# Value, key and query projections of a hybrid encoder layer as three products over high and low halves, the low halves by GpSimd

## The reference

```
xn = rmsnorm(h, norm_mix_g)
proj = xn @ w_in                      # 2048 x 3584
a = proj[..., :2048]                  # gated convolution (GLU)
q, k, v = 1024, 256 and 256 columns   # attention, rope on q and k
glu = a[..., :1024] * sigmoid(a[..., 1024:])
y = depthwise conv of glu, 31 taps    # then layernorm, silu
mn = rmsnorm(mem, norm_mem_g)         # 256 memory tokens
mk, mv = mn @ w_ck, mn @ w_cv
```

## Time and profile before

| what | us |
|---|---|
| median of 3 runs | 2055.32 |
| lowest and highest run | 2044.23 and 2055.69 |
| the profiled execution | 2047.77 |
| its span, first to last instruction | 2046.0 |

### The profile page before, as it was taken

How to read it: one execution, slowest core, us unless ns; L and a number is a source line. 1 busy time by engine, 2 the same in 40 slices (tenths; PEclk the granted TensorE clock), 3 DMA queues, 4 the chain that set the end, 5 groups by cost and what they waited for, 6 DMA issues and landing times. The chain is left out here.

```text
span 2046.0 us, 29568 instructions
## 1 busy us (share of the span) xinstructions
PE 1981.8 (97%) x11192; PEld 1765.1 (86%) x11192; DVE 1530.7 (75%) x2436; ACT 858.1 (42%) x857; POOL 718.3 (35%) x504
## 2 busy tenths in 40 slices
PE   7999998999899999999999999999999999999997
PEld 6987776998799999999999889988888888888886
DVE  5988745456678788989988987567677777778875
ACT  4340136334334554455454435433434343334343
POOL 2010110220726677587787875011001011114300
PEclk9999998999899999999999999999999999999999
DMA  5464393443344787788888787779998989998983
GB/s 207 164 193 141 116 400 137 153 168 123 127 137 156 247 275 268 272 281 286 274 272 298 265 306 283 294 274 348 340 343 328 343 326 349 364 360 345 372 314 136
DMA packets 101226, 531.27 MB, mean 260 GB/s; under 512 B 19376, under 2 KB 21568, under 8 KB 45792
## 3 DMA queue, kind: packets, MB, share of 16 engines
q1 hardware_dynamic: 71552, 408.93, 55.8%
q0 software_dynamic: 24304, 106.45, 14.4%
q10 hardware_dynamic: 5296, 14.98, 1.9%
HBM read 491.34 MB, written 38.14 MB: 259 GB/s over the span
## 5 line engine op out<-in xcount | busy, mean ns | idle before, releaser
L889 DVE TENSOR_TENSOR wl<-raw,wh 128x2048 fp32r<-128x2048 f32 x310 | 712.4, 2299 | 287.1 <-ACT wh L519 275.5
L519 ACT ACTIVATE wh<-raw 128x2048 fp32r<-128x2048 f32 x310 | 593.3, 1915 | 572.5 <-DMA raw<-in_v 408.4
L1537 PE MATMUL acc<-xhl,wh 128*128 128x448 f32 x2048 | 648.9, 377 | 12.2 <-DVE wl L889 12.2
L1538 PE MATMUL acc<-xhl,wl 128*128 128x224 f32 x2048 | 542.8, 265 | 0.0
L1537 PEld LDWEIGHTS acc<-xhl,wh 128*128 128x128 f32 x2048 | 386.7, 189 | 44.7 <-DVE wl L889 14.6
L1538 PEld LDWEIGHTS acc<-xhl,wl 128*128 128x128 f32 x2048 | 393.2, 192 | 0.0
L2025 POOL DMA_INDIRECT G<-gsum,cell x224 | 348.2, 1554 | 99.7 <-issue 74.8
L1514 PE MATMUL acc<-xhl,wh 128*128 128x288 f32 x768 | 231.7, 302 | 14.8 <-DVE wl L925 14.2
L1515 PE MATMUL acc<-xhl,wh 128*128 128x288 f32 x768 | 228.4, 297 | 0.0
L1516 PE MATMUL acc<-xhl,wl 128*128 128x288 f32 x768 | 227.9, 297 | 0.0
L1514 PEld LDWEIGHTS acc<-xhl,wh 128*128 128x128 f32 x768 | 146.5, 191 | 18.2 <-DVE wl L925 14.2
(11 more groups left out here) (306 smaller groups left out, 2638.8 us busy)
## 6 DMA issues: line engine op xcount, KB each, us to landing
raw<-in_u SPq DMA_DIRECT2D x128, 1024.0 KB
raw<-in_v SPq DMA_DIRECT2D x128, 1024.0 KB
raw<-in_w_mix SPq DMA_DIRECT2D x28, 1024.0 KB
G<-zero SPq DMA_DIRECT2D x16, 1024.0 KB, 13.8
raw<-in_w_out SPq DMA_DIRECT2D x16, 1024.0 KB
raw<-in_w_pq SPq DMA_DIRECT2D x16, 1024.0 KB
gin<-G SPq DMA_DIRECT2D x32, 512.0 KB
h<-hbg ACTq DMA_DIRECT2D x32, 448.0 KB
```

Of the source, the lines that this page charges most:

```text
L519: act.activation(wh[:, n % 4], raw[:, n % 4], ACT.Copy).then_inc(hi_done, 1)
L889: dve.tensor_tensor(wl[:, n % 4], raw[:, n % 4], wh[:, n % 4].bitcast(F32), ALU.subtract).then_inc(lo_done, 1)
L1537: pe.matmul(acc[:, s, 0:2 * NU], wh[:, s, j, :], xu[:, j, 0:2 * NU], start=(j == 0), stop=False)
L1538: ins = pe.matmul(acc[:, s, 0:NU], wl[:, s, j, :], xuh[:, j, :], start=False, stop=(j == DT - 1))
```

## The change

The plain float32 products of the 12 value, key and query slots become three products over `wh`, `wl`, `xh` and `xl`. ScalarE makes the 12 high halves, which were not made before, GpSimd makes the 12 low halves with one subtraction of 128 x 2048 elements each, into `wl`. `xg` and its 16 copies are gone. The memory tokens are loaded into a tile of their own where `xg` was; the squares and the scaled copy `memg` lie over `wh` and are made when slots 9, 10 and 11 of the stage have been used. GpSimd's sums of convolution tiles move between its subtractions, and its two cache loads wait for the scaled memory tokens.

```diff
-            memsq, memT = sb(o, "memsq", [P, DT, MEM]), sb(o, "memT", [P, DT, MEM])
+            memsq, memg = sb(o, "memsq", [P, DT, MEM]), sb(o, "memg", [P, DT, MEM])
...
-                    xg = sb(o1, "xg", [P, DT, N])
+                    memT = sb(o1, "memT", [P, DT, MEM])
...
+        vkq_lo = sem("vkq_lo")
...
-            def glu_iteration(i, first=False, last=False):
+            def glu_iteration(i, first=False):
                 for s in range(4):
-                    if not (last and s >= 4 - AHEAD):
-                        hi_next(GLU0, i, s)
-                    if last:
-                        for t in range(4 * s, 4 * s + 4):
-                            act.activation(xg[:, t, :], hT[:, t, :], ACT.Copy, scale=par[:, Q_GMIX + t:Q_GMIX + t + 1]).then_inc(xg_ready, 1)
+                    hi_next(GLU0, i, s)
...
             act.wait_ge(lo_done, VKQ0)
-            act.sem_inc(hi_done, OUT0 - VKQ0)
+
+            for n in range(12 - AHEAD):
+                hi_next(VKQ0, 0, n)
+            act.wait_ge(vkq_lo, 12)
+            act.sem_inc(hi_done, OUT0 - MEM0)
+            act.wait_ge(slot_used, VKQ0 + 10)
             for n in range(4):
                 at = slice(4 * n, 4 * n + 4)
                 act.wait_ge(mem_in[n], 16)
                 act.activation(memsq[:, at, :], memT[:, at, :], ACT.Square).then_inc(mem_sq, 1)
-                act.wait_ge(mem_sq, n + 1)
+            for n in range(4):
+                act.wait_ge(slot_used, VKQ0 + 11 + n // 2)
                 for m in range(4 * n, 4 * n + 4):
-                    ins = act.activation(memT[:, m, :], memT[:, m, :], ACT.Copy, scale=par[:, Q_GMEM + m:Q_GMEM + m + 1])
+                    ins = act.activation(memg[:, m, :], memT[:, m, :], ACT.Copy, scale=par[:, Q_GMEM + m:Q_GMEM + m + 1])
                 ins.then_inc(mem_ready, 1)
 
+            act.wait_ge(mem_sq, 4)
+            act.wait_ge(mem_ready, 4)
...
             for n in range(12):
-                pe.wait_ge(raw_in[n % 4], 16 * (VKQ0 // 4 + n // 4 + 1))
+                pe.wait_ge(vkq_lo, n + 1)
                 pe.wait_ge(acc_free, VKQ0 + n + 1)
                 for j in range(DT):
-                    if n == 0 and j % 4 == 0:
-                        pe.wait_ge(xg_ready, j + 4)
-                    ins = pe.matmul(acc[:, n % 4, 0:N], raw[:, n % 4, j, :], xg[:, j, :], start=(j == 0), stop=(j == DT - 1))
+                    pe.matmul(acc[:, n % 4, 0:N], wh[:, n % 4, j, :], xh[:, j, :], start=(j == 0), stop=False)
+                    pe.matmul(acc[:, n % 4, 0:N], wh[:, n % 4, j, :], xl[:, j, :], start=False, stop=False)
+                    ins = pe.matmul(acc[:, n % 4, 0:N], wl[:, n % 4, j, :], xh[:, j, :], start=False, stop=(j == DT - 1))
                 ins.then_inc(slot_used, 1)
...
+            def weight_lo(n):
+
+                pool.wait_ge(hi_done, VKQ0 + n + 1)
+                pool.tensor_tensor(wl[:, n % 4], raw[:, n % 4], wh[:, n % 4].bitcast(F32), ALU.subtract).then_inc(vkq_lo, 1)
+
+            for n in range(AHEAD):
+                weight_lo(n)
             pool.wait_ge(acc_free, VKQ0 + 4)
             pool.wait_ge(hist_zero, 1)
             pool.wait_ge(hist_in, 16)
             pool.dma_start(dr["nconv_p"], glu[:, :, NP_:NP_ + HIST]).then_inc(early_out, 16)
             pool.dma_start(dr["nconv_s"], glu[:, :, XW - HIST:XW]).then_inc(early_out, 16)
-            for t in range(1, CT - 1):
+
+            def ln_part(t):
+
                 pool.wait_ge(conv_dve, t + 1)
...
+            for n in range(AHEAD, 12):
+                weight_lo(n)
+                if n % 2 == 1:
+                    ln_part(n // 2)
+            for t in range(12 // 2, CT - 1):
+                ln_part(t)
             pool.wait_ge(slot_used, MEM0)
+            pool.wait_ge(mem_ready, 4)
```

More of the change, by code:

```diff
@@ L322, in build @@
         x_in = [sem(f"x_in{n}") for n in range(4)]
-        xg_ready = sem("xg_ready")
         mem_sq, mem_ready, mem_stat = sem("mem_sq"), sem("mem_ready"), sem("mem_stat")
@@ L559, in _ @@
             glu_iteration(0, True)
-            with act.Fori(1, 3) as i:
+            with act.Fori(1, 4) as i:
                 glu_iteration(i)
-            glu_iteration(3, last=True)
             act.wait_ge(lo_done, VKQ0)
-            act.sem_inc(hi_done, OUT0 - VKQ0)
+            for n in range(12 - AHEAD):
[3 more added lines that the diff above has]
+            act.wait_ge(slot_used, VKQ0 + 10)
             for n in range(4):
@@ L1656, in mem_part @@
                         pe.wait_ge(mem_ready, j // 4 + 1)
-                    ins = pe.matmul(acc[:, 2 + m % 2, 0:MEM], raw[:, m % 4, j, :], memT[:, j, :], start=(j == 0), stop=(j == DT - 1))
+                    ins = pe.matmul(acc[:, 2 + m % 2, 0:MEM], raw[:, m % 4, j, :], memg[:, j, :], start=(j == 0), stop=(j == DT - 1))
                 if part == 3:
```

## The result

| | before | changed |
|---|---|---|
| median us | 2055.07 (4 runs, 2044.23 to 2055.69) | 2090.69 (4 runs, 2088.91 to 2093.68) |
| profiled execution: span | 2046.0 | 2089.0 |
| rope's first instruction | 228.01 | 265.42 |

The ratio is 1.0187, with a 95% interval of 1.0167 to 1.0206: slower by 1.7 to 2.1%, some 38 us. It is estimated from all runs; the two medians alone differ by 35.6 us. The number on record was 2090.

What follows compares the result with a forecast made beforehand. TensorE set the pace, but VectorE ended the stage: 12 x 4.45 us lost to GpSimd's subtractions less 13.75 of waits is 39.7; 2047.8 + 39.7 + 2.2 (clock) = 2090 us, range 2072 to 2108.

Steps and rivals of the forecast that it cites:

- The point to follow: End of the value, key and query stage: rope's start, 228.01 us before, was put at 267.7, 39.7 us later.
- the short pairs: Overlapping VectorE and GpSimd instructions before the change: VectorE lost GpSimd's duration less about 0.15 us, as 0.65 of 0.81.
- TensorE off the path: In the 12 slots: products fall from 7.78 to 6.29 us a slot; gain beyond VectorE's 13.2 us of waits doesn't count.
- What is queued behind: Behind GpSimd's subtractions: five convolution sums and two DMA issues move back, nothing waiting; TensorE waits from fourth or fifth slot.
- The memory tokens: Squares after slot 9, last eight scaled copies (3.4 us) after slot 11, ending before the last evacuation: price nothing.
- The clock: Transposes and products before rope's third rotation: after idling some 15 us, TensorE runs at half speed, +2.2 us on rope.
- The clock rival: In the 12 slots: waits keep TensorE at 1.2 GHz, 11.5 us a slot, rope 45.7 us late, 2096 us; chance 12%.
- Behind rope: Everything after rope: all later work moves by the same amount, with nothing added but the clock's 2.2 us.
- Where the low halves go: GpSimd's output: said to go into `wl` and not over `raw`, making nothing longer or shorter.
- no exclusion: Convolution steps beside a subtraction: GpSimd lets VectorE in between, stage ends about 10.7 us earlier, 2037 us; chance 5%.
- a dearer rounded output: GpSimd's subtraction: writing the rounded type costs more, up to 6.9 us each, 2117 us; chance 9%.

## Why the prediction was right, step by step

*The point to follow.* Rope's start was put at 267.7 and came at 265.42. Between the steps at 122.95 and rope VectorE had 105.06 us before, 13.75 of them waits, so 91.3 of work; after, from 122.61, it had 142.81 and no wait for TensorE. It lost 51.5 us to the 12 subtractions, **4.29 each where 4.45 were taken**. The instruction is 4.68 us, at the upper end of the 4.55 to 4.67 worked out from shorter ones, where 4.6 were taken. The loss is smaller than the instruction by 0.39, where the short pairs gave 0.15. The step at 184.81 shows how: it began 0.15 us after the subtraction and ended 0.19 after it (at 189.53 to 189.34), where alone it takes 0.37, so 4.35 of 4.68 us were lost. Besides, evacuations from PSUM go on, but only one fell beside a subtraction: at 214.08, in the middle of GpSimd's work from 209.32 to 218.58, it took its usual time. That leaves part of the 0.39 untraced.

```profile
214.08 0.41 DVE L996 TENSOR_TENSOR qch<-acc,rstd 128x256 f32<-128x256 f32 x1
```

That term was mis-sized by 12 x 0.16 = 1.9 us; the stage also began 0.34 us earlier. Together they are the 2.3 us. The Trainium skill, GPSIMD Engine Reference, section "Elementwise — side-by-side cycle accounting", had 4497 ns for this size; the measurement, 4677, decides, and is 4% more.

*TensorE off the path.* Right, and shown: with a third of its products gone the time stays. The fifth slot was named as the first to wait for a bank, and it was, at 159.68; TensorE waited for VectorE five times in the stage, for 22.3 us.

*What is queued behind.* One step of this part failed, at no cost. The five sums of convolution tiles were said to move behind the subtractions with nothing waiting for them. But GpSimd's queue is in order, and each sum first waits for VectorE to finish a tile: 14.62 us before 183.90, 13.76 before 208.56. The subtractions behind them waited as well, so that slots 8 and 10 got their low halves late. It cost nothing because TensorE, which needs them, was held up longer by the banks: slot 10 began at 214.74, when its bank was free, 0.8 us after its low half. Had VectorE been the faster engine, these waits might have bound the stage; no run shows that.

*The memory tokens.* Nothing, as predicted. The squares and copies on ScalarE in the changed kernel end at 243.37, and the last evacuation, for which all else waits, comes at 258.45:

```profile
240.07 3.30 ACT L572 ACTIVATE memg<-memT,par 128x256 f32<-128x256 f32 x8 [3.03 <-PE acc L1566]
```

*The clock.* 2.2 us were put on the third rotation. It waited 2.63 us for TensorE instead of 0.53, 2.1 more. TensorE was idle for 19.08 us ahead of the transposes. In its windows, with busy time (count) and granted clock, one sees the lower of its two levels (1.2 GHz) from 243.60 on, and five microseconds of work at that level.

```profile
243.60:259.00 15.40, 0.00 (x0) 0.50 0.10 35
259.00:264.00 5.00, 4.89 (x18) 0.50 0.00 0
264.00:272.00 8.00, 8.00 (x40) 1.00 0.00 0
```

The clock rival, lower level through the stage, did not come: 0.70 to 0.96 were granted on average in the 20 us stretches from 140 to 240, and even where it was lower, TensorE had time. VectorE was busy for 19.9 to 20.0 us of each of these stretches.

*Behind rope.* Nothing was put there. The third rotation is 39.5 us later than before, the first of line 1975's products (line 1996 now) 40.6, and the transposes of line 1839 (1842) 43.1:

```profile
L1996 POOL TENSOR_TENSOR xn<-hT,rstd x4: 2385/3422/4547, 588.6 to 599.8; 128x1024 f32<-128x1024 f32 x4
```

The 1.1 us in the first stretch and 2.5 in the second are not explained by the runs. From rope to these transposes it is 1059.8 us before and 1065.5 in the changed kernel, but 1074.4 with two split slots and 1061.1 with four, so that stretch differs by up to 15 us between single executions; 2.5 us there say nothing. It is part of the luck, though: the profiled execution grew by 43 us where 42 were forecast, the 2.3 us too many at rope being outweighed by 3.6 behind it for which nothing was put.

*Where the low halves go.* The prediction says that they go into `wl` and not over `raw`. That was a misreading: the scope of `raw` has ended where `wl` is declared, and both have one place in SBUF, so the subtraction does overwrite `raw`. Nothing of the sum hung on it. The extra subtractions added to the kernel before, which write into a tile apart from their sources, took the same 4.68 us.

The 7.5 us between the profiled execution and the median of before were left out of the forecast; the ratio, 1.0187, gives 38 us and not 42. Neither rival given 5% (no exclusion) and 9% (a dearer rounded output) came: steps were shut out by every subtraction, and none took over 4.86 us. One outcome does not say whether these chances were well chosen.

## What to carry to other kernels

Before work is moved from VectorE to GpSimd, look in the trace for a pair of their SBUF instructions that overlap, and see whether one is longer by the other's time. If it is, price the move by GpSimd's duration on VectorE's clock, here 4.3 us for work that VectorE does itself in 2.1. It came free here only beside VectorE's evacuations from PSUM and, where GpSimd read nothing, beside VectorE's steps with two SBUF inputs. Cutting the instruction in pieces bought nothing. And when a near-second engine has 1.1 us a slot to spare, a faster leader is worth only that: split the slots that the spare time pays for, and no more.

## What the runs showed that I had not expected

GpSimd does not always get the next turn. Against the kernel before, where a 288-element sum takes about 0.80 us beside back-to-back convolution steps, the same sum took 3.85, 1.85 and 1.90 us in the kernel where GpSimd only fills, and 1.95 and 2.79 with the low halves on VectorE, the last beside a subtraction of 2.28. Six or seven steps of VectorE passed in the first case while GpSimd waited. GpSimd in order of time there:

```profile
138.31 3.85 POOL L1931 TENSOR_TENSOR sqsum<-y 128x288 f32<-128x288 f32 x1
...
163.19 0.81 POOL L1931 TENSOR_TENSOR sqsum<-sqsum,y 128x288 f32<-128x288 f32 x1
...
175.57 1.85 POOL L1931 TENSOR_TENSOR sqsum<-sqsum,y 128x288 f32<-128x288 f32 x1
```

What decides who goes next was not tried. Also new: a step with one SBUF input, the `tensor_scalar` of line 951, is shut out like those with two, 4.72 us instead of 0.37, and one of line 949 was shut out even by a fill, which left the steps with two inputs alone.
